# Decays of a state-space layer: one matmul per half of the heads, and the copy of B times C moved to VectorE

## The reference, cut to what matters

```python
cs = jnp.cumsum(dA_c, axis=1)                       # per chunk and head
seg = cs[:, :, None] - cs[:, None, :]
decay = jnp.exp(jnp.where(causal, seg, -jnp.inf))
cb = jnp.einsum('bign,bjgn->bgij', c_c, b_c)
y_intra = jnp.einsum('bgij,bijgh,bjghp->bighp', cb, decay, xdt_c)
```

## Time and profile before

| | |
|---|---|
| time, median of 3 runs | 2509.05 us (2507.21 to 2511.1) |
| the profiled execution: its time | 2510.24 us |
| its span in the profile | 2508.4 us |
| TensorE busy | 2453.4 us, 98% |
| VectorE busy | 1609.6 us, 64% |
| ScalarE busy | 1123.3 us, 45% |
| GpSimd busy | 41.8 us, 2% |
| TensorE clock granted, mean | 0.994 |
| moved by DMA | 446.26 MB, 178 GB/s |

### The profile page before, as it was taken

The page is one execution under the profiler, slowest core; times in us unless marked ns, Lnnn a source line. Parts: engine busy times, 40 slices in busy tenths (PEclk is TensorE's granted clock), DMA queues, the critical chain, the costliest instruction groups (busy, mean ns, idle before and its releaser), DMA issues.

```text
span 2508.4 us, 34093 instructions
## 1 busy us (share of the span) xinstructions
PE 2453.4 (98%) x12538; PEld 2077.8 (83%) x12538; DVE 1609.6 (64%) x2180; ACT 1123.3 (45%) x1562; POOL 41.8 (2%) x75
## 2 busy tenths in 40 slices
PE   7999999999999999999999999999899999999998
PEld 6888888888887888888888878888788888888886
DVE  6777777776558646556556567555774565664655
ACT  4444444444435434435444444444553443443442
POOL 1000000000000000000000000000000000000000
PEclk9999999999999999999999999999999999999999
DMA  7655555544647666566566536325565655655653
GB/s 214 178 159 160 159 159 161 156 151 165 209 156 212 224 193 186 191 192 190 193 190 188 192 127 214 108 103 186 150 222 191 191 187 193 189 193 192 188 191 113
DMA packets 498774, 446.26 MB, mean 178 GB/s; under 512 B 13616, under 2 KB 376288, under 8 KB 497360
## 3 DMA queue, kind: packets, MB, share of 16 engines
q1 hardware_dynamic: 496896, 433.61, 55.6%
q0 software_dynamic: 1744, 10.81, 1.2%
HBM read 442.26 MB, written 2.10 MB: 177 GB/s over the span
## 4 chain that ended last, share of the span: by engine, by line
PE 94%; DVE 3%; issue 1%; ACT 1%; DMA 1%; POOL 0%; SPq 0%; DVEq 0%; ACTq 0%; POOLq 0%
PE ps L432 26%; PE ps L450 15%; PE ps L452 15%; PE ps L451 15%; PE ps L434 13%; PE ps L503 2%; PE ps L587 1%; PE ps L482 1%; PE ps L484 1%; PE ps L483 1%; DVE wlo L1216 1%; PE ps L728 1%; ACT whi L815 1%; PE ps L708 1%; DMA xin<-in_x 1%
## 5 line engine op out<-in xcount | busy, mean ns | idle before, releaser
L1216 DVE TENSOR_TENSOR wlo<-raw,whi 128x1024 fp32r<-128x1024 f32 x818 | 997.7, 1224 | 619.1 <-ACT whi L815 609.3
L815 ACT ACTIVATE whi<-raw 128x1024 fp32r<-128x1024 f32 x818 | 861.8, 1057 | 757.9 <-PE ps L452 486.0
L432 PE MATMUL ps<-actA,whi 128*128 128x512 f32 x2832 | 1006.9, 400 | 7.7 <-DVE wlo L1216 4.9
L434 PE MATMUL ps<-actA,wlo 128*128 128x256 f32 x2832 | 794.2, 280 | 0.0
L432 PEld LDWEIGHTS ps<-actA,whi 128*128 128x128 f32 x2832 | 533.9, 189 | 139.5 <-issue 7.7
L434 PEld LDWEIGHTS ps<-actA,wlo 128*128 128x128 f32 x2832 | 536.4, 189 | 2.1 <-issue 1.7
L450 PE MATMUL ps<-whi,actB 128*128 128x512 f32 x1056 | 412.6, 391 | 0.0
L452 PE MATMUL ps<-whi,actB 128*128 128x512 f32 x1056 | 411.0, 389 | 0.0
L451 PE MATMUL ps<-wlo,actB 128*128 128x512 f32 x1056 | 410.9, 389 | 0.0
L452 PEld LDWEIGHTS ps<-whi,actB 128*128 128x128 f32 x1056 | 198.2, 188 | 41.6
L450 PEld LDWEIGHTS ps<-whi,actB 128*128 128x128 f32 x1056 | 198.3, 188 | 40.8
(11 more groups left out here) (216 smaller groups left out, 1702.1 us busy)
## 6 DMA issues: line engine op xcount, KB each, us to landing
raw<-in_mlp_w SPq DMA_DIRECT2D x512, 512.0 KB, 3.9
raw<-in_a_w_in SPq DMA_DIRECT2D x162, 512.0 KB, 4.0
raw<-in_a_w_out SPq DMA_DIRECT2D x64, 512.0 KB, 3.9
raw<-in_b_w_q SPq DMA_DIRECT2D x32, 512.0 KB, 4.3
raw<-in_b_w_o SPq DMA_DIRECT2D x32, 512.0 KB, 3.5
raw<-in_kv_w SPq DMA_DIRECT2D x16, 512.0 KB, 3.5
gb<-in_ln_g POOLq DMA_DIRECT2D x4, 1024.0 KB, 6.8
gb<-in_ln_b POOLq DMA_DIRECT2D x4, 1024.0 KB, 9.6
```

What stands on the lines that cost most here:

```text
L432: e.matmul(ps[:, b, :].rearrange("p (a n) -> p a n", a=2), whi[:, s, w], act[:, kt, :, :], start=(kt == 0), stop=False)
L434: last = e.matmul(ps[:, b, T:2 * T], wlo[:, s, w], act[:, kt, 0, :], start=False, stop=(kt == KT - 1))
L815: e.activation(whi[:, s, :], raw[:, r, :], ACT.Copy).then_inc(w_hi_done, C.up(w_hi_done))
L1216: e.tensor_tensor(wlo[:, s, :], raw[:, r, :], whi[:, s, :].bitcast(F32), ALU.subtract).then_inc(w_split, C.up(w_split))
```

## The change

The cumulative sums are brought into one layout in which a single product gives the exponent of four heads. `csrc` holds, for each head, the rounded sum, its rest and two ones (and in a second copy two ones and both negated); eight transposes instead of two turn it into `csx` and `css`. For each group and chunk GpSimd multiplies `csx` by a selection of rows, `selg`, into `csm`, and `seg` is one product of `css` with it. There is no mask in the product any more: ACT writes max(-x, 0) of both banks to `em` (Relu with scale -1) and then takes the exponential of the negative over all 1024 columns; the non-causal half becomes 1 or less and is cleared because `bc_out` multiplies C-B by a triangle of ones. `bc_out` is on DVE, directly behind the convolution of row tile 0, and takes the place of ACT's copy. GpSimd selects twice per group, each time as soon as the `seg` pair before has read `csm`, and `s3` waits for its selection too. `cross` writes to `xpad` itself, without `crossb`. At the last group `silu(5, 1)` moves ahead of a weight step.

```diff
             def cs_transposes():
                 e.wait_ge(cs_split, C.next(cs_split))
-                transposes(6, [cshl[:, c, :, :].rearrange("p a n -> p (a n)") for c in range(NH)])
+                for k in range(2):
+                    transposes(6 + k, [csrc[:, k, c, 4 * i:4 * i + 4, :, :].rearrange("p g a n -> p (g a n)")
+                                       for c in range(NH) for i in range(2)])
...
             def seg(c, hh, b):
                 fill(b)
-                o = ps[:, b, :].rearrange("p (h n) -> p h n", h=4)
-                e.matmul(o, ident_r[:, :], smask_r[:, :].unsqueeze(1).broadcast_to([P, 4, P]), start=True, stop=False)
-                e.matmul(o, ncs2[:, c, :], sel8[:, 4 * hh:4 * hh + 4, :], start=False, stop=False)
-                for h in range(4):
-                    last = e.matmul(ps[:, b, h * P:(h + 1) * P], sel8[:, 4 * hh + h, :], cs2[:, c, :],
-                                    start=False, stop=(h == 3))
-                last.then_inc(full[b], C.up(full[b]))
+                e.matmul(ps[:, b, :].rearrange("p (h n) -> p h n", h=4), css[:, c, 0, :], csm[:, 4 * hh:4 * hh + 4, :],
+                         start=True, stop=True).then_inc(full[b], C.up(full[b]))
...
             def s3():
+                e.wait_ge(heads_selected, C.next(heads_selected))
                 seg(1, 0, 7)
                 seg(1, 1, 6)
...
             def decay(c):
                 for hh, b in ((0, 7), (1, 6)):
                     e.wait_ge(full[b], C.next(full[b]))
-                    e.activation(em[:, c, hh * BLK:(hh + 1) * BLK], ps[:, b, :], ACT.Exp).then_inc(free[b], C.up(free[b]))
+                    e.activation(em[:, c, hh * BLK:(hh + 1) * BLK], ps[:, b, :], ACT.Relu, scale=-1.0).then_inc(
+                        free[b], C.up(free[b]))
+                for b in (7, 6):
+                    e.wait_ge(free[b], C.now(free[b]))
+                e.activation(em[:, c, :], em[:, c, :], ACT.Exp, scale=-1.0).then_inc(decayed, C.up(decayed))
...
             e.memset(xpad[:, :, 0:3], 0.0)
+            e.memset(csrc[:, :, :, :, :, :].rearrange("p k c g a n -> p (k c g a n)"), 1.0)
...
-                e.tensor_tensor(xpad[:, x, 3:3 + T], ps[:, x, 0:T], crossb[:, x, :], ALU.add).then_inc(
+                e.tensor_tensor(xpad[:, x, 3:3 + T], ps[:, x, 0:T], xpad[:, x, 3:3 + T], ALU.add).then_inc(
...
+            def bc_out():
+                e.wait_ge(full[6], C.next(full[6]))
+                e.tensor_copy(bcb[:, 0, :], ps[:, 6, 0:P])
+                e.tensor_tensor(bcb[:, 1:3, :], ps[:, 6, P:3 * P].rearrange("p (c n) -> p c n", c=NH),
+                                tri[:, :].unsqueeze(1).broadcast_to([P, NH, P]), ALU.mult).then_inc(
+                                    free[6], C.up(free[6]))
...
                 conv(0, par)
+                bc_out()
                 step()
...
+            silu(5, 1)
             step()
-            silu(5, 1)
-            split_y(0)
+            split_y(0, {1: bc_out})
...
-            def select(g):
-                e.tensor_copy(sel8[:, :, :], sel2[:, bass.ds(g * GH, GH)].unsqueeze(2)
-                                          .broadcast_to([P, GH, P])).then_inc(heads_selected, C.up(heads_selected))
+            def select(g, c):
+                i = g // 4
+                e.tensor_tensor(csm[:, :, :], csx[:, c, i, :].bitcast(F32).unsqueeze(1).broadcast_to([P, GH, P]),
+                                selg[:, (g % 4) * GH:(g % 4 + 1) * GH].unsqueeze(2).broadcast_to([P, GH, P]),
+                                ALU.mult).then_inc(heads_selected, C.up(heads_selected))
+
+            def seg_read(g, c):
+                e.wait_ge(full[6], 3 + 4 * g + 2 + c)
...
+            select(0, 0)
+            for g in range(NG):
+                seg_read(g, 0)
+                select(g, 1)
+                if g + 1 < NG:
+                    seg_read(g, 1)
+                    if g == 3:
+                        e.tensor_copy(css[:, :, 0, :], css[:, :, 1, :])
+                    select(g + 1, 0)
                 e.wait_ge(y_squared, C.next(y_squared, 2))
                 group_rstd()
```

More of the change, by code:

```diff
@@ L847, in _ @@
                 split_weights()
-            C.n[full[6]] += 1
-            C.n[full[7]] += 1
+            for b in (6, 7):
+                C.n[full[b]] += 1
+                C.n[free[b]] += 1
             def constants_out():
@@ L877, in dt_cs2, with cross, mlp_cross @@
                 e.wait_ge(full[6], C.next(full[6]))
[L878 to L883, removed]
-                products()
-                e.activation(buf[:, i % 2, :], ps[:, b0 + i % 2, T:2 * T], ACT.Copy).then_inc(cross_out, C.up(cross_out))
+                e.activation(csx[:, :, :, :].rearrange("p c t n -> p (c t n)"), ps[:, 6, :], ACT.Copy).then_inc(
+                    free[6], C.up(free[6]))
+                e.wait_ge(full[7], C.next(full[7]))
+                e.activation(css[:, :, :, :].rearrange("p c t n -> p (c t n)"), ps[:, 7, :], ACT.Copy).then_inc(
+                    free[7], C.up(free[7]))
+                e.wait_ge(free[6], C.now(free[6]))
+                e.wait_ge(free[7], C.now(free[7]))
+                e.activation(var, ident[:, 0:2], ACT.Copy, scale=0.0).then_inc(cs_turned, C.up(cs_turned))
+            def cross(i):
+                products()
+                e.activation(xpad[:, i % 2, 3:3 + T], ps[:, i % 2, T:2 * T], ACT.Copy).then_inc(
+                    cross_out, C.up(cross_out))
+            def mlp_cross(i):
+                products()
+                e.activation(mcross[:, i % 2, :], ps[:, 4 + i % 2, T:2 * T], ACT.Copy).then_inc(
+                    cross_out, C.up(cross_out))
             def tanh(i):
@@ L898, in a1 @@
             def a1():
-                e.wait_ge(full[6], C.next(full[6]))
-                e.activation(bcb[:, :, :].rearrange("p a n -> p (a n)"), ps[:, 6, 0:3 * P], ACT.Copy).then_inc(
-                    free[6], C.up(free[6]))
+                C.n[full[6]] += 1
+                C.n[free[6]] += 1
             def decay(c):
@@ L1322, in dt_sums @@
                 e.wait_ge(cs_ready, C.now(cs_ready))
-                e.tensor_copy(cshl[:, :, 0, :], csr[:, :, :].bitcast(F32))
-                e.tensor_tensor(cshl[:, :, 1, :], cs.rearrange("p (c h) -> p c h", c=NH),
-                                             csr[:, :, :].bitcast(F32), ALU.subtract).then_inc(cs_split, C.up(cs_split))
+                hi_cs = csr[:, :, :].bitcast(F32).rearrange("p c (g n) -> p c g n", n=GH)
+                all_cs = cs.rearrange("p (c g n) -> p c g n", c=NH, n=GH)
+                e.tensor_copy(csrc[:, 0, :, :, 0, :], hi_cs)
+                e.tensor_tensor(csrc[:, 0, :, :, 1, :], all_cs, hi_cs, ALU.subtract)
+                e.tensor_scalar(csrc[:, 1, :, :, 2, :], hi_cs, -1.0, None, ALU.mult)
+                e.tensor_tensor(csrc[:, 1, :, :, 3, :], hi_cs, all_cs, ALU.subtract).then_inc(cs_split, C.up(cs_split))
+                C.n[free[7]] += 1
+                C.n[full[7]] += 1
                 C.n[free[5]] += 1
@@ L1372, in d1 @@
                         xdt_ready, C.up(xdt_ready))
+            def bc_out():
[3 more added lines that the diff above has]
+                                tri[:, :].unsqueeze(1).broadcast_to([P, NH, P]), ALU.mult).then_inc(
+                                    free[6], C.up(free[6]))
             def d23(c):
[L1375 to L1378, removed]
+                e.wait_ge(decayed, C.next(decayed))
+                for b in (6, 7):
+                    C.n[free[b]] += 1
+                    C.n[full[b]] += 1
                 x = em[:, c, :].rearrange("p (h n) -> p h n", h=GH)
@@ L1501, in _, with split_y @@
                 group(2 * i + 3, 1)
-            def split_y(half):
+            def split_y(half, after={}):
                 act = act1 if half else actA
@@ L1908, in _ @@
             e.wait_ge(selection_ready, C.next(selection_ready))
-            e.memset(var, 0.0).then_inc(pool_step, C.up(pool_step))
-            select(0)
-            def turn(g):
-                e.wait_ge(m_ready, C.next(m_ready, 2))
-                select(g)
+            e.wait_ge(cs_turned, C.next(cs_turned))
+            select(0, 0)
[7 more added lines that the diff above has]
+                    select(g + 1, 0)
                 e.wait_ge(y_squared, C.next(y_squared, 2))
                 group_rstd()
-            before = dict(C.n)
-            turn(1)
-            with C.loop(NG - 2, before, 1) as i:
-                turn(i + 2)
-            e.wait_ge(m_ready, C.next(m_ready, 2))
-            e.wait_ge(y_squared, C.next(y_squared, 2))
-            group_rstd()
             e.wait_ge(yT_done, C.next(yT_done))
```

35 lines of the change are left out of this document (19 added, 16 removed).

## The result

| | before | after |
|---|---|---|
| median of 17 runs each, us | 2510.23 | 2514.36 |
| lowest to highest, us | 2505.07 to 2513.12 | 2511.26 to 2520.07 |
| profiled execution, its time / span, us | 2510.24 / 2508.4 | 2516.87 / 2515.0 |

What follows compares the result with a forecast made beforehand. TensorE was taken as bound by 1.9 us per group, then DVE's chain. Start -0.26 and +0.7, first group -0.3, five periods +6.0, seventh +1.5, last stage -2.54 and -0.25: +4.8, 2513.9 us; range 2497 to 2525.

Steps and rivals of the forecast that it cites:

- Period 67.9: Repeating group of the state-space stage: claimed to take 67.9 us against 66.65, +1.2.
- The old chain: DVE and ACT work of a group before the change: claimed to need 64.8 us, 1.9 below TensorE's 66.65.
- The work added to it: DVE and ACT per group: bc_out +0.54, Exp about +0.8, less the old pass's hold of 0.83; together +0.5 us.
- The two holds: GpSimd's two selections per group make DVE instructions wait: 1.07 us for the first, 1.5 us for the second.
- The pass of two inputs: One GpSimd selection over two inputs of 1024 elements: claimed to hold DVE's SBUF reads for 1.95 us.
- Which instruction is held: DVE in each group: first selection delays L1216 (L1230 after the change) by 1.07 us, second delays L1340 by 1.5.
- The first groups: Start: -0.26 and +0.7 us; first full group: second selection falls into DVE's idle time, period 66.4, -0.3.
- The last stage: Seventh group and last stage: second hold +1.5 us, TensorE's two shorter pairs -2.54, silu(5) moved ahead -0.25.
- A: Rival on GpSimd: the hold is 0.83 us or none, total -5.7 or -10.5 us, 2498.5 to 2503.4; chance 0.24.
- B: Rival: dearer holds, 2.8 and 3.5 us per group, +27, 2536; or ACT table loads, some +15; chance 0.15.
- C: Rival: the DVE/ACT chain does not bind and TensorE keeps its whole saving, -20.1 us, 2489; chance 0.08.
- D: Rival: s3 waits for a selection longer than 5.4 us, which paces TensorE; time above B's; no chance given.

Runs made afterwards that it cites:

- e1: Kernel before with only the first of the six state-space decay products in each half, so decays are not computed: 2497.11 us, ratio 0.9948.
- e2: Kernel after with each GpSimd selection but the first replaced by a copy of 8 elements, so decays are wrong: 2499.42 us, ratio 0.9952.
- e3: Kernel after with each selection but the first made as a one-input copy of the same 128x1024 elements, decays wrong: 2505.84 us, ratio 0.9977.
- e8: Kernel after, unchanged, run once more: 2513.76 us, ratio to before 1.0016.
- padded kernel: Kernel after with five dummy TensorE products in each half of the decays ahead of the one that counts: 2509.77 us, ratio 1.0005.
- e9: Kernel after with the second chunk's selection in two halves and the other selection behind the sixth convolution: 2510.01 us, ratio 1.0000.

## Why the prediction was right

By its steps.

- **Period 67.9:** 67.80. It came out of three terms of which none was quite right. The old chain was put at 64.8 us and needs 64.4 or less (e1). The work added to it was put at +0.5, 0.54 for `bc_out` and 0.8 for Exp less the 0.83 that the old pass held; measured are 0.79, 1.16 and 0.84, so +1.1, which makes 65.5 against the 65.46 of e2. The two holds were put at 1.07 and 1.5 = 2.57 us; in the profile they are 1.95 to 3.3 us, 2.7 on average, of which 2.3 reach the period. Two terms were too large and one too small: 64.8 + 0.5 + 2.6 against 64.4 + 1.1 + 2.3. That they cancel to 0.1 us is luck. (The recorded 310.15 for the end of the second pass should be 308.3 + 1.95 = 310.25, which makes its hold 1.6; it changes nothing else.)
- **The pass of two inputs:** 1.95 us was put together from other rows, 1.90 is measured, and the estimate of 2.2 us was too long. The 1.85 us that I gave to the pass of one input held a wait (e3 has 1.04). The 0.82 us from a pair's start to the pass, with 0.18 in it for which no row stood, are 0.70 (376.31 to 377.01).
- **Which instruction is held:** the second pass, L1360, as forecast. For the first I had named L1230; that holds in groups 2 and 3 only. From group 4 on (in the second profile of the same kernel, e8, in groups 5 and 7) the pass finds L1230 already issued, waits for it, and holds the silu, for 1.70 us instead of 1.07. A microsecond in the starting times decides, and mine were not that exact. I had also put the holds down to two SBUF inputs; the tensor-scalar L1360 has one (so has L1340) and is held as well.
- **The first groups:** forecast +0.44 for the start and -0.3 for the first full group. Measured +0.8 and +2.7. In the first full group both passes hold VectorE (L1391 at 108.00 by 0.9 us, L1367 at 113.27 by 1.7), where I had given the second one idle time; without holds (`e2_select_tiny`) this group is 0.5 us longer than before, so about 2.2 of the 2.7 are theirs. This is the step that failed, by 3 us.
- **The last stage:** from the start of group 7 to the first addition to the residual it is 116.1 us against 117.4, -1.3; forecast +1.5 - 2.54 - 0.25 = -1.3. The wait of 2.62 us did not shrink, though: it is 2.87 us at 569.44, and 2.83 more follow at 573.92 for `actA`. The sum of the stage came out for another reason than the one given.
- **Cancelled by the rest:** behind the last stage the kernel after is 2.7 us shorter (1895.7 against 1898.3) in code that the change leaves as it was, but for where two buffers lie. The ten profiled executions of kernels made from it besides the two of it give 1893.9 to 1898.0, the two with the code of before 1897.5 and 1898.3. Without it the forecast would have been 3 us too low by the medians. Whether it is scatter is open. So the period, which is the heart of the forecast, was right by its mechanism; the total to within a microsecond is luck, since the start and the first full group cost over 4 us more than forecast and this stretch gave 2.7 back.
- **Rivals:** A (short holds) would need passes of 1.04 us; e3 made them and gained 4.8 us, close to A's 5.7. B needed dearer holds or table loads on ScalarE: the kernel after has a single table load, as before, and holds of 2.7 us, not 6.3. C (TensorE keeps all, 20.1 us) is not reached even where TensorE's saving stands alone: e1 has 13.5 us. D would show as TensorE waiting for a selection; no such wait is in the first 620 us. The padded kernel shows that TensorE's saving is worth nothing in the kernel after.
- **What should show it:** passes 7 and 14 us behind `s1`, held neighbours, waits released by `xT`, `xpad` and `em`: all there. TensorE's idle time is 1.7 to 2.4 us a group and not 3 to 4; 0.3 us of the rest are in TensorE's floor, 64.4 instead of 64.1. What makes up the other 1.4 us, in which its records show it busy, is not shown: the clock is not the answer, as the group from 164.26 on has 1.8 us of idle time, a clock of 1.00 and 67.86 us.

Not settled: a placement that holds nobody and delays no powers (the pass behind the fifth convolution, with the late Exp) was not tried; by the account above, as an estimate, it would reach TensorE's floor (65.46 - 1.16 = 64.3 us).

## What to carry to other kernels

When the leading engine is relieved, the next chain must be priced with everything that the same change puts into it; here TensorE's 2.2 us a group were there to be had (e1), and a product on GpSimd, an Exp and a masked copy took back 3.4. A GpSimd pass is paid by VectorE, so look at which instructions stand beside it (two SBUF inputs or a tensor-scalar: held; an input in PSUM: not) and also at what stands behind it on GpSimd itself. Where an engine has got slack, giving it useless work need lose nothing (here it even gained 4 to 5 us, because the passes fell elsewhere), and this is a cheap test of who the bound is.

## What the runs showed of the hardware

The recorded span of a GpSimd instruction holds its wait for VectorE: the same selection is recorded with 1.90, 2.65, 2.79 and 2.92 us. So a pass is priced by its shortest record.

The granted clock fell in groups with small idle pieces, 0.3 to 1.0 us each. These two windows are the same group, of the kernel after and of its second run (the first row is of the kernel after):

```profile
232.10:299.20 67.10, 64.72 (x341) 54.35 (x340) 53.22 (x77) 31.80 (x48) 4.88 (x5) 0.97 0.55 156
```

```profile
231.50:299.10 67.60, 65.11 (x350) 54.42 (x349) 53.22 (x77) 31.83 (x48) 4.88 (x5) 1.00 0.56 156
```

The figure is a mean between the two levels of 1.2 and 2.4 GHz. With nearly the same idle time, 2.4 and 2.5 us, it is 0.97 in one and 1.00 in the other, and the groups of e9, with 1.6 to 2.3 us, show 1.00 throughout. So the sum of the idle time alone does not decide it. The slower clock costs nothing here: over both runs the periods at 0.97 or 0.98 average 67.8 us (seven), those at 1.00 too (three), which fits that VectorE's chain sets them.
